# Half of the first modulation as one-column products on TensorE, with the condition and the first chunk loaded ahead of the rest

## The reference, cut to what matters

```python
cs = silu(c)                                    # c: 1 x 1024
mod = (cs @ ada_w[l] + ada_b[l]).reshape(B, 3, 3, D)
h = rmsnorm(x, norm_g[l, 0]) * (1 + mod[:, 0, 1]) + mod[:, 0, 0]
x = x + 0.5 * mod[:, 0, 2] * swiglu(h, w_gate, w_up, w_down)
```

## Time and profile before

| | |
|---|---|
| median of 3 runs | 3071.79 us (3070.0 to 3074.74) |
| profiled execution | 3076.41 us |
| its span | 3074.3 us |
| PE busy | 2939.0 us, 96% of the span |
| PEld busy | 2585.7 us, 84% |
| DVE busy | 1586.9 us, 52% |
| ACT busy | 608.9 us, 20% |
| DMA | 733.17 MB, mean 238 GB/s |

### The profile page before, as it was taken

The page is one execution under the profiler, slowest core; times in us unless marked ns, Lnnn a source line. Parts: engine busy times, 40 slices in busy tenths (PEclk is TensorE's granted clock), DMA queues, the critical chain, the costliest instruction groups (busy, mean ns, idle before and its releaser), DMA issues.

```text
span 3074.3 us, 68427 instructions
## 1 busy us (share of the span) xinstructions
PE 2939.0 (96%) x28798; PEld 2585.7 (84%) x28799; DVE 1586.9 (52%) x3012; ACT 608.9 (20%) x1439; POOL 15.6 (1%) x27
## 2 busy tenths in 40 slices
PE   5999999999999999999999989997999999999999
PEld 4999888899999989889999779986786668766875
DVE  6776662376677667326767458899421112111212
ACT  1111104121111211412112302135212101210121
POOL 0000000000000000000000000000000000000000
PEclk9999999999999999999999999998999999999999
DMA  7665654355466565534556347832287898889885
GB/s 306 255 248 192 260 216 188 137 193 206 193 250 243 220 246 220 199 113 190 213 213 233 127 180 301 322 145 83 105 328 296 315 368 344 328 317 368 344 330 202
DMA packets 55543, 733.17 MB, mean 238 GB/s; under 512 B 6608, under 2 KB 6792, under 8 KB 10804
## 3 DMA queue, kind: packets, MB, share of 16 engines
q1 hardware_dynamic: 51364, 716.68, 59.9%
q0 software_dynamic: 3984, 13.74, 1.3%
HBM read 729.31 MB, written 4.23 MB: 239 GB/s over the span
## 4 chain that ended last, share of the span: by engine, by line
PE 82%; DMA 11%; DVE 5%; issue 1%; ACT 1%; SPq 0%; DVEq 0%; ACTq 0%
PE psum L728 35%; PE psum L819 17%; PE psum L1358 10%; PE psum L1314 9%; DMA ring<-in_up_e_dram 4%; PE psum L806 3%; PE psum L722 2%; DMA ring<-in_up_dram 2%; DMA ring<-in_down_e_dram 1%; PE psum L1374 1%; DMA ring<-in_w_v_dram 1%; DVE ring L1866 1%; DMA ring<-in_w_ccch_dram 1%; PE psum L1339 1%; DMA ring<-in_ada_dram 1%
## 5 line engine op out<-in xcount | busy, mean ns | idle before, releaser
L1314 PE MATMUL psum<-h_t,ring 128*64 128x88 f32 x11264 | 436.5, 239 | 16.5 <-DMA ring<-in_up_e_dram 16.1
L1314 PEld LDWEIGHTS psum<-h_t,ring 128*64 128x64 f32 x11264 | 430.2, 137 | 22.2 <-issue 21.1
L728 PE MATMUL psum<-work,ring 128*128 128x128 f32 x3680 | 440.8, 275 | 2.2 <-ACT work L1447 2.2
L728 PEld LDWEIGHTS psum<-work,ring 128*128 128x128 f32 x3680 | 425.2, 192 | 3.1 <-issue 1.6
L728 PE MATMUL psum<-work 128*128 128x128 f32 x3328 | 388.9, 275 | 2.0 <-issue 1.0
L728 PEld LDWEIGHTS psum<-work 128*128 128x128 f32 x3328 | 380.0, 192 | 2.6 <-issue 2.0
L1866 DVE SCALAR_TENSOR_TENSOR ring<-ring,cond 128x1024 f32<-128x1024 f32 x240 | 279.3, 1219 | 86.7 <-DMA ring<-in_ada_dram 86.6
L1358 PE MATMUL psum<-ring,work 128*88 128x512 f32 x704 | 304.0, 593 | 2.4 <-DMA ring<-in_down_e_dram 2.4
L819 PE MATMUL psum<-work,ring 128*128 128x256 f32 x1344 | 296.2, 383 | 4.8 <-DMA ring<-in_m_out_dram 3.1
L819 PEld LDWEIGHTS psum<-work,ring 128*128 128x128 f32 x1344 | 257.4, 192 | 42.2 <-DMA ring<-in_m_out_dram 3.9
L819 PE MATMUL psum<-h_t,ring 128*128 128x256 f32 x1280 | 278.8, 380 | 1.0 <-ACT h_t L1568 1.0
(11 more groups left out here) (378 smaller groups left out, 2538.8 us busy)
## 6 DMA issues: line engine op xcount, KB each, us to landing
ring<-in_up_e_dram SPq DMA_DIRECT2D x64, 2048.0 KB, 8.3
ring<-in_ada_dram SPq DMA_DIRECT2D x60, 2048.0 KB, 8.0
ring<-in_up_dram SPq DMA_DIRECT2D x55, 2048.0 KB, 8.7
ring<-in_down_e_dram SPq DMA_DIRECT2D x32, 1792.0 KB, 8.1
ring<-in_down_dram SPq DMA_DIRECT2D x20, 2816.0 KB, 10.3
ring<-in_up_e_dram SPq DMA_DIRECT2D x32, 1536.0 KB, 8.9
ring<-in_down_e_dram SPq DMA_DIRECT2D x16, 2048.0 KB, 8.3
ring<-in_w_qk_dram SPq DMA_DIRECT2D x12, 2048.0 KB, 8.2
```

The costliest lines, as they stand in the source:

```text
L728: mm = pe.matmul(bank(bank_of)[:, pair * P:(pair + 1) * P], w, right(i), start=(first and pair == 0 and i == 0), stop=(pair == lin.pairs - ...
L1314: mm = pe.matmul(half(b)[lo:hi, 0:width], w[:, lo:hi], h[:, k, 0:width], start=(k == 0), stop=(k == lin.depth - 1))
```

## The change

It touches the prologue. SP issues the load of `cond` first, then the first chunk of `ada0`, then the eight small loads, then the other three chunks. Each chunk of `ada0` now has its two halves in different layouts: two output columns are summed by VectorE as before, the other two are made on TensorE by 16 products per chunk whose moving operand is one column of the condition. To have the condition as columns (`cond_t`), TensorE first multiplies `cond` by a single one, 128 values at a time (8 products), and VectorE copies the result. Between these pieces TensorE runs products of `ones` by `ones`: 12, 4, 8, 5, 5, 5 and 4 of them. VectorE makes the scale after two chunks and the tiles `raw` right then, but tells TensorE of them only after the fourth chunk. GpSimd writes the bias table only after the first chunk of `up0` has been used.

```diff
@@ sync engine
+            sp.dma_start(cond[:, :], bass.AP(dram["cond"].tensor, 0, [[0, P], [1, D]])).then_inc(first_cond_in, 16)
...
                         sp.wait_ge(chunk_done[slot], use + 1)
                         sp.dma_start(ring[:, slot, 0:width], src).then_inc(chunk_in[slot], 16)
+                        if p.name == "ada0" and n == 0:
+                            small_loads()
@@ tensor engine
+            def products_of_ones(b, many):
+
+                for _ in range(many):
+                    pe.matmul(bank(b)[:, 0:P], ones[:, :], ones[:, :], start=True, stop=True)
+
+            def first_ada(j, ahead):
+
+                p, b = place("ada_pe"), ADA_BANKS[j]
+                pe.wait_ge(bank_free[b], reads(p, b))
+                products_of_ones(b, ahead)
+                slot = chunk_landed(place("ada0").slot(j))
+                for m in range(2):
+                    for k in range(DT):
+                        mm = pe.matmul(psum[:, b * 512 + m:b * 512 + m + 1],
+                                       ring[:, slot, (2 + m) * D + k * P:(2 + m) * D + (k + 1) * P],
+                                       cond_t[:, k:k + 1], start=(k == 0), stop=(k == DT - 1))
+                mm.then_inc(bank_full[b], 1)
+
+            p = place("cond_cols")
+            pe.wait_ge(ones_set, 1)
+            pe.wait_ge(bank_free[7], reads(p, 7))
+            products_of_ones(7, 12)
+            pe.wait_ge(signal["cond_set"], 1)
+            for k in range(DT):
+                mm = pe.matmul(psum[:, 7 * 512 + k:7 * 512 + k + 1], cond[0:1, k * P:(k + 1) * P], ones[0:1, 0:1],
+                               start=True, stop=True)
+            mm.then_inc(bank_full[7], 1)
+            pe.wait_ge(bank_free[7], reads(p, 7) + 1)
+            first_ada(0, 4)
+
+            pe.wait_ge(bank_free[0], reads(place("load_x"), 0))
+            products_of_ones(0, 8)
             pe.wait_ge(small_in, 128)
...
-            pe.wait_ge(ones_set, 1)
+            for j in range(1, 4):
+                first_ada(j, 5)
+            pe.wait_ge(bank_free[0], reads(place("up0", 0), 0))
+            products_of_ones(0, 4)
@@ scalar engine
+            act.wait_ge(first_cond_in, 16)
+            act.activation(cond[:, :], cond[:, :], ACT.Silu).then_inc(signal["cond_set"], 1)
             act.wait_ge(small_in, 128)
-            act.wait_ge(signal["cond_in"], place("ada0").of("cond_in", 0))
-            act.activation(cond[:, :], cond[:, :], ACT.Silu).then_inc(signal["cond_set"], 1)
@@ vector engine
+            def first_ada(j):
+
+                b, (slot, use) = ADA_BANKS[j], place("ada0").slot(j)
+                dve.wait_ge(chunk_in[slot], use * 16 + 16)
+                for m in range(2):
+                    w = ring[:, slot, m * D:(m + 1) * D]
+                    dve.scalar_tensor_tensor(w, w, 1.0, cond[:, :], ALU.mult, ALU.mult,
+                                             accum_out=ada_acc[:, 4 * j + m:4 * j + m + 1]).then_inc(dve_done, steps.one())
+                dve.wait_ge(bank_full[b], products(place("ada_pe"), b))
+                dve.tensor_copy(ada_acc[:, 4 * j + 2:4 * j + 4], psum[:, b * 512:b * 512 + 2]).then_inc(chunk_done[slot], 1)
...
+            first_ada(1)
+            first_mod(new_scale, ada_b(0, 1, 2)[0], 0)
+            prepare_gain(vcol("norm_g", 0, DT))
+            for f in range(DT):
+                dve.tensor_scalar(raw[:, f, 0:S], x[:, f, :], gain[:, f:f + 1], None, ALU.mult).then_inc(dve_done, steps.one())
+            first_ada(2)
             for f in range(1, DT - 1):
                 squares_so_far(place("norm0", 0), f)
...
+            first_ada(3)
+            first_mod(new_shift, ada_b(0, 0, 1)[0], DT)
+            prepare_shift()
+            dve.sem_inc(signal["raw"], DT)
             dve.wait_ge(rows_out, 16)
@@ gpsimd
-            load_cond(0)
             pool.memset(ones[:, :], 1.0).then_inc(ones_set, 1)
...
+            slot, use = place("up0", 0).slot(0)
+            pool.wait_ge(chunk_done[slot], use + 2)
@@ layout of the weights (host)
+    ada[0:4, :, 2 * D:4 * D] = by_tile(a["ada_w"][0], 4)[SCALE_FIRST[0:4]][:, :, 2 * D:4 * D]
```

More of the change, by code:

```diff
@@ L57 @@
 NARROW = 88
+ADA_BANKS = (5, 6, 7, 4)
 TRIOS = ((0, 1, 2), (3, 4, 5), (6, 7, 2))
@@ L198, in stages @@
     prologue = {
-        "load_x": with_(uses(b0=1, b1=1, b2=1, b3=1), cond_in=16, cond_set=1, x_tile=DT),
+        "cond_cols": uses(b7=1),
+        "load_x": with_(uses(b0=1, b1=1, b2=1, b3=1), cond_set=1, x_tile=DT),
         "bias_rows": uses(b4=1),
+        "ada_pe": uses(b4=1, b5=1, b6=1, b7=1),
         "ada0": Linear(0, 4, 32 * P, "none", adas=4),
@@ L506, in build @@
         cols = small[:, 212:216]
+        cond_t = small[:, 0:DT]
         share = flat(36, 4).rearrange("p (m s) -> p m s", m=MIX)
@@ L579, in build @@
         small_in = sem("small_in")
+        first_cond_in = sem("first_cond_in")
         ones_set = sem("ones_set")
@@ L640, in _, with small_loads @@
         def _(sp):
-            for dst, src in ((x_tok, dram["x"]), (ident[:, :], dram["ident"]), (vec[:, :], dram["vec"]),
-                             (one_hot, dram["one_hot"]), (off_mask, dram["off_mask"]),
-                             (table, dram["rel_bias"]),
-                             (bgate[:, :], dram["b_gates"]),
-                             (iota8[:, :], dram["iota8"])):
-                sp.dma_start(dst, src).then_inc(small_in, 16)
+            def small_loads():
+                for dst, src in ((x_tok, dram["x"]), (ident[:, :], dram["ident"]), (vec[:, :], dram["vec"]),
+                                 (one_hot, dram["one_hot"]), (off_mask, dram["off_mask"]),
+                                 (table, dram["rel_bias"]),
+                                 (bgate[:, :], dram["b_gates"]),
+                                 (iota8[:, :], dram["iota8"])):
+                    sp.dma_start(dst, src).then_inc(small_in, 16)
+            sp.dma_start(cond[:, :], bass.AP(dram["cond"].tensor, 0, [[0, P], [1, D]])).then_inc(first_cond_in, 16)
             def stream(p):
@@ L2407, in combine, with first_mod @@
                     dve.sem_inc(bank_free[b], 1)
+            def first_ada(j):
[7 more added lines that the diff above has]
+                dve.tensor_copy(ada_acc[:, 4 * j + 2:4 * j + 4], psum[:, b * 512:b * 512 + 2]).then_inc(chunk_done[slot], 1)
+                dve.wait_ge(chunk_done[slot], use + 2)
+                dve.sem_inc(bank_free[b], 1)
+            def first_mod(to, bias_of, a):
+                dve.wait_ge(dve_done, steps.count())
+                dve.tensor_tensor(to, ada_acc[:, a:a + DT], bias_of, ALU.add).then_inc(dve_done, steps.one())
+                dve.wait_ge(dve_done, steps.count())
+            p = place("cond_cols")
+            dve.wait_ge(bank_full[7], products(p, 7))
+            dve.tensor_copy(cond_t, psum[:, 7 * 512:7 * 512 + DT]).then_inc(bank_free[7], 1)
+            dve.wait_ge(signal["cond_set"], 1)
+            first_ada(0)
             dve.wait_ge(small_in, 128)
@@ L2420, in _ @@
                               ALU.add).then_inc(bank_free[4], 1)
+            first_ada(1)
[4 more added lines that the diff above has]
+            first_ada(2)
             for f in range(1, DT - 1):
                 squares_so_far(place("norm0", 0), f)
-            p = place("ada0")
-            dve.wait_ge(signal["cond_set"], p.of("cond_set", 0))
-            walk(p, loop(p), None, ada_sums(p))
-            ada_next(p, (new_scale, *ada_b(0, 1, 2)), (new_shift, *ada_b(0, 0, 1)))
+            first_ada(3)
+            first_mod(new_shift, ada_b(0, 0, 1)[0], DT)
+            prepare_shift()
+            dve.sem_inc(signal["raw"], DT)
             dve.wait_ge(rows_out, 16)
-            prepare(vcol("norm_g", 0, DT))
-            for f in range(DT):
-                raw_tile(f)
             for l in steps.loop("layer", DEPTH):
@@ L3235, in layout @@
     two = range(DEPTH)
+    ada = cat([by_output(w)[order] for name, orders in (("ada_w", (LAYER_ADA, LAYER_ADA)),
+                                                        ("ada_w_2", (MIXER_ADA, list(range(12)))))
+               for w, order in zip(a[name], orders)])
+    ada[0:4, :, 2 * D:4 * D] = by_tile(a["ada_w"][0], 4)[SCALE_FIRST[0:4]][:, :, 2 * D:4 * D]
     arrays = {
@@ L3241, in layout @@
         "cond": np.concatenate([a["c"], a["c_2"]], axis=0),
-        "ada": cat([by_output(w)[order] for name, orders in (("ada_w", (LAYER_ADA, LAYER_ADA)),
-                                                             ("ada_w_2", (MIXER_ADA, list(range(12)))))
-                    for w, order in zip(a[name], orders)]),
+        "ada": ada,
         "up": cat([paired(a["ffn_w_gate"][l, n], a["ffn_w_up"][l, n]) for l in two for n in range(2)]),
```

## The result

The changed kernel takes 3160.02 us (median of 4, 3148.66 to 3179.71) against 3073.26 us before (3070.0 to 3074.85), a ratio of 1.029 with an interval of 1.0238 to 1.0343: slower by 87 us, where 7.9 were forecast. The profiled execution took 3161.48 us, its span is 3159.4.

The account below looks back on a forecast made before the run. The prediction took the start's chain of waits, then TensorE, as the bound: first feed-forward product 9.1 us later, 1.2 back, +7.9 on the 3071.8 median, giving 3079.7 us. Its 8-in-10 range was 3061.5 to 3085.5.

Parts of the forecast that it names:

- The part on the start: Prologue up to the first feed-forward product: TensorE's added work makes it 9.1 us later, 1.2 back, sum +7.9 us.
- Ones at half: TensorE's opening 24 passes of ones by ones at half clock: 5.1 us, ending at 7.5 us.
- bias rows: TensorE's bias rows after the transposes: 0.7 us at full clock, ending at 25.1; clock rise expected at 23.6, mid-transposes.
- second chunk: Second `ada0` chunk on TensorE: ones 1.1 us, one-column passes at full clock 3.4, two at half 0.5, ending at 30.1.
- third and fourth: Third and fourth `ada0` chunks on TensorE at half clock: 9.3 us each, ending at 48.7.
- First L817: First feed-forward product, L806 in the kernel before: start at 50.4 us, 9.1 us later than 41.26.
- The one-column pass at the half clock: TensorE's one-column products in the `ada0` chunks: taken as 225 ns, bounds 114 to 228.
- Rival A: TensorE in the prologue: products of ones hold the clock at full, total 3061.8 us; chance 0.24.
- Rival B: TensorE in the prologue: weight loads do not slow with the clock, total 3068.7 to 3072.0 us; chance 0.10.
- C: TensorE in the prologue: the clock never rises between pieces, +16.1 us, total 3087.9 us; chance 0.06.
- D: First feed-forward: bias table stalls a chunk of `up0`, TensorE waits 2.7 us once or twice, up to 3085.1; chance 0.04.
- The step that failed: From the first feed-forward product to the kernel's end: any shift of that product moves the end equally.

Follow-up runs that it names:

- 216: Kernel before, and changed kernel, each with TensorE's expert-loop head padded to slot 216 of its 256-instruction block: 3131.73 us (1.0189) and 3141.23 us (1.022).
- slot 192: Kernel before with the head of TensorE's expert loop padded to slot 192 of its 256-instruction block: 3105.82 us, ratio 1.0119.
- slots 64 and 232: Kernel before with TensorE's expert-loop head padded to instruction 64 or 232 of its 256-instruction block: 3071.39 us (0.9991) and 3180.07 us (1.0356).
- slots 64 and 128: Kernel before with TensorE's expert-loop head padded to instruction 64 or 128 of its 256-instruction block: 3071.39 us (0.9991) and 3073.33 us (1.0002).
- slot 0: Kernel before with the head of TensorE's expert loop padded to the first instruction of a 256-instruction block: 3081.35 us, ratio 1.002.
- after_slot0: Changed kernel with the head of TensorE's expert loop padded to the first instruction of a 256-instruction block: 3083.94 us, ratio 1.004.

## Why the prediction was wrong

**The part on the start was right in its mechanism, nearly step by step.** Ones at half to 7.5 (7.3), columns of the condition to 9.3 (9.1), first chunk to 17.9 (17.2), ones to 21.3 (20.8), bias rows to 25.1 (23.3: 16 transposes took 1.76 us, all at full pace, so the rise came by 20.8 and not at 23.6), second chunk to 30.1 (28.5, its last four passes at half where two were forecast), third and fourth 9.3 each (8.96). First L817 at 50.4 (48.3); by the end of the first chunk the change costs 5.6 us, not 7.9. The one-column pass at the half clock, taken as 225 ns from the weight loads of the earlier trace rows, is 207; that was the unknown with the widest bounds, and its upper part was right. Rival A failed: the windows' clock column reads 0.50 in chunks three and four, with TensorE busy throughout. Rival B failed by the 207. C failed at the transposes. D came true once, 2.0 us for 2.7. That 5.6 and 2.0 make 7.6, next to the 7.9 of the sum, is luck: the sum had no stall of a chunk in it.

The page that the prediction named at rival A asks to keep TensorE busy (the Trainium skill, TensorE: Matmul & The Clock Gate, the table on why this matters for kernels). The runs show the price of following it with ones: 7.2 us of the start, and the clock low all the same in three chunks of four (0.53, 0.50, 0.50).

**The step that failed** is the one that carries the start's sum to the end of the kernel: "So whatever moves the first L806 moves the end by the same amount." Its reason was that TensorE hardly waits from 41.26 on. That takes it, without a reason, that work which the change does not touch keeps its time. The expert loop is such work, and in the profile it grew by 65 us, with 5 more right behind it, because the instructions put ahead of it moved its place. The rows that would have given warning were there: the wait of 6.41 us for "issue" at L1331, once in seven turns, in a loop with 1996 instructions and a jump; and the queue of instructions on the page. Neither was read, as neither stood near the change. With the loop pinned where it is quick, the measured cost of the change is 10.9 us, and its 3084.2 us would have been inside the predicted range, near the top.

The range failed with it: every case in it was a case of the start. A case "some loop falls on the wrong side of a block's edge" had to stand there, with a price of one gap per turn from the row above, 7 times 6.4 or more, 45 us and up.

**What stays open.** The shift between the own places and the slots; why some turns at the same place are quick and others not (two of seven long gaps at 216, five of seven in the changed kernel, none in the profile of slot 192); and what the store does inside. The smaller differences between the changed kernel and the kernel before ahead of the loop (14.8 us there, of which 7.6 are explained) stand in single profiles and were not followed. The kernels that differ from the kernel before only in the loop reach it between 2224 and 2233 us, those of the changed kernel between 2242 and 2246.

## What to carry to other kernels

Instructions added anywhere move all later code of that engine, and a long loop with a jump in it can go from no fetching at all to fetching all of its blocks in each turn. After every edit compare the packets of the instruction queue and the waits for "issue" at the loops' heads; if they changed, pin the loop or put the branch that is taken next to the loop's end before you judge the edit. And filler work on an engine is queued work: it delays whatever lands while it runs, so count it as a wait, and take it only if a run shows the clock that it buys.

## What was not expected of the hardware

A turn of the same loop costs 100 to 117 us, and the same kernel 3071 or 3180 us by where the loop's code lies (slots 64 and 232). A turn between two long gaps fetches 8 to 10 blocks of 16 KB again, a quick one at most one, mostly none. Padding that is jumped over once cost nothing that these runs can tell at slots 64 and 128; slot 0 measured 1.002 (1.0008 to 1.0032), outside its expectation. Its profile has one wait more, 3.9 us for "issue" ahead of the loop's first product; whether that is the padding's price is not shown, and after_slot0 has no such wait. One-column float32 passes slow down with the clock, from 112 to 213 ns from start to start, and 32 of them without a gap leave the clock low (6.6 us, 0.50 in the windows of the third and fourth chunk) or let it fall (at 27.5, in the second), while 16 transposes behind ones ran at full pace, and without ones the clock rose during them.
